# Three-pass scores and a split projection in differential attention, and scores between the two maps' transposes in forgetting attention

## The reference, cut to what matters

```python
def forgetting_attention(q, k, v, fg_logit):        # per head
    s = einsum(q_block, k) * ATT_SCALE + cum[q] - cum[k]
    s = where(ki <= qi, s, NEG)
    out = softmax(s) @ v

def diff_attention(q, k, v, lam):                   # per head: q, k hold two maps of width 64
    sc = einsum(q_block, k) * scale                 # two maps
    p = softmax(where(mask, sc, neg))
    w = p[map 0] - lam * p[map 1]
    out = w @ v
```

## Time and profile before

| what | value |
|---|---|
| median of 3 runs | 2993.35 us (2993.19 to 2996.78) |
| the profiled execution's own time | 2991.64 us |
| its span, first to last instruction | 2990.0 us |
| mean granted TensorE clock | 0.988 |
| PE busy | 2814.2 us, 94% of the span |
| DVE busy | 1602.3 us, 54% |
| ACT busy | 655.7 us, 22% |
| a head of forgetting attention in the loop | 85.66 us |
| a head of differential attention in the loop | 72.96 us |

### The profile page before, as it was taken

How to read it: one execution, slowest core, us unless ns; L and a number is a source line. 1 busy time by engine, 2 the same in 40 slices (tenths; PEclk the granted TensorE clock), 3 DMA queues, 4 the chain that set the end, 5 groups by cost and what they waited for, 6 DMA issues and landing times.

```text
span 2990.0 us, 35245 instructions
## 1 busy us (share of the span) xinstructions
PE 2814.2 (94%) x13336; PEld 2222.8 (74%) x13336; DVE 1602.3 (54%) x2058; ACT 655.7 (22%) x1157; POOL 299.7 (10%) x295
## 2 busy tenths in 40 slices
PE   6889999989999999999999999999998999999996
PEld 4757776868888888877888888888866777777664
DVE  5664446364454555555454554445374666666644
ACT  3133224031111111112110111011032333333321
POOL 0599800000000000001000000000000000000000
PEclk9999999999999999999999999999999999999998
DMA  4211110324343434433222222222242222222131
GB/s 148 85 57 57 42 54 20 138 99 169 112 159 135 154 132 163 154 111 130 83 73 82 83 71 84 84 84 70 85 155 98 72 72 72 70 70 72 52 113 70
DMA packets 48617, 286.59 MB, mean 96 GB/s; under 512 B 6576, under 2 KB 6704, under 8 KB 18608
## 3 DMA queue, kind: packets, MB, share of 16 engines
q1 hardware_dynamic: 22064, 119.01, 11.6%
q0 software_dynamic: 14544, 105.91, 10.2%
q10 hardware_dynamic: 11952, 60.89, 5.3%
HBM read 248.03 MB, written 29.36 MB: 93 GB/s over the span
## 4 chain that ended last, share of the span: by engine, by line
PE 79%; DVE 12%; issue 4%; ACT 2%; DMA 1%; DVEq 0%; SPq 0%; ACTq 0%
PE PB L239 11%; PE PB L241 11%; PE PB L240 11%; PE OBB L239 8%; PE OBB L241 8%; PE OBB L240 8%; PE TBB L754 3%; PE OBB L842 3%; PE PB L800 3%; PE TBB L239 2%; PE TBB L240 2%; PE TBB L241 2%; DVE small L1010 1%; DVE on L1820 1%; DVE cacc L1196 1%
## 5 line engine op out<-in xcount | busy, mean ns | idle before, releaser
L239 PE MATMUL PB<-HH,WH 128*128 128x512 f32 x1520 | 599.9, 395 | 23.9 <-issue 7.7
L241 PE MATMUL PB<-HH,WL 128*128 128x512 f32 x1520 | 595.2, 392 | 0.0
L240 PE MATMUL PB<-HL,WH 128*128 128x512 f32 x1520 | 595.1, 392 | 0.0
L239 PE MATMUL OBB<-HH,WH 128*128 128x512 f32 x992 | 400.0, 403 | 0.9 <-DVE WL L255 0.9
L241 PE MATMUL OBB<-HH,WL 128*128 128x512 f32 x992 | 387.7, 391 | 0.0
L240 PE MATMUL OBB<-HL,WH 128*128 128x512 f32 x992 | 387.0, 390 | 0.0
L239 PEld LDWEIGHTS PB<-HH,WH 128*128 128x128 f32 x1520 | 287.5, 189 | 91.5 <-issue 27.2
L240 PEld LDWEIGHTS PB<-HL,WH 128*128 128x128 f32 x1520 | 287.6, 189 | 61.8 <-issue 2.2
L241 PEld LDWEIGHTS PB<-HH,WL 128*128 128x128 f32 x1520 | 287.1, 189 | 59.7
L255 DVE TENSOR_TENSOR WL<-RAW,WH 128x2048 fp32r<-128x2048 f32 x101 | 234.1, 2318 | 60.8 <-DMA WH<-units 44.1
L2058 POOL DMA_DIRECT2D WH<-units x85 | 45.5, 535 | 2009.6 <-PE PB L239 1320.1
(11 more groups left out here) (314 smaller groups left out, 3743.9 us busy)
## 6 DMA issues: line engine op xcount, KB each, us to landing
WH<-units POOLq DMA_DIRECT2D x85, 1024.0 KB, 5.0
RAW<-units SPq DMA_DIRECT2D x85, 1024.0 KB, 4.7
gs<-units ACTq DMA_DIRECT2D x16, 1024.0 KB, 4.8
gu<-gs ACTq DMA_DIRECT2D x16, 1024.0 KB, 3.9
RAW<-gu SPq DMA_DIRECT2D x16, 1024.0 KB, 4.8
WH<-gu POOLq DMA_DIRECT2D x16, 1024.0 KB, 5.3
tmpd<-xr SPq DMA_DIRECT2D x128, 64.0 KB, 2.0
A<-xT SPq DMA_DIRECT2D x4, 1024.0 KB, 12.5
```

The lines of the kernel that those rows point to most:

```text
L239: first = pe.e.matmul(out, wh, xh, start=start, stop=False)
L240: pe.e.matmul(out, wh, xl, start=False, stop=False)
L241: return pe.e.matmul(out, wl, xh, start=False, stop=stop), first
```

## The change

In differential attention q and k of a head are split into high and low parts (`qh`, `ql`, `kh`, `kl`, float32r), and the scores are three float32r matmuls in place of one float32 matmul, at least 256 columns wide. The copies `qT` and `kT` go; `qh` and `kh` are made by ACT and `ql` and `kl` by DVE (`low_scores`), all in block 7. A part of a projection that ends in a block keeps its last two contraction tiles (6 matmuls, `TAIL`) for a place between `scores(t + 1)` and `values(t)`. ACT copies a projection out of `DB` between the two exponentials; DVE copies a gate after both maxima. The `low_part` at a head's end moves behind `at1`.

In forgetting attention `scores(t + 1)` and the square sums go between the transposes of the first and of the second map; up to block 3 the maps have a bank each. `maximum(t + 1, 0)` goes before the second map's copies, and the norm's Ln and Exp (`root_of`) between the two exponentials.

```diff
@@ scores(t) @@
-                for b in range(0, n, HALF):
+                for b in range(0, n if not forget else 0, HALF):
+                    w = max(256, min(HALF, n - b))
+                    for q_part, k_part in ((qh, kh), (qh, kl), (ql, kh)):
+                        for c in range(2):
+                            rows = slice(64 * c, 64 * c + 64)
+                            pe.e.matmul(PB[c][:, b:b + w], q_part[rows, t * P:(t + 1) * P],
+                                        k_part[rows, b:b + w], start=q_part is qh and k_part is kh,
+                                        stop=False, skip_group_check=True)
+                for b in range(0, n if forget else 0, HALF):
@@ turn(t) becomes turn(t, c) @@
+            def turn_bank(t, c, g):
+                return TB[c if forget and t < 4 else g]
@@ projections @@
+            TAIL = 6
+            def projections(t, tail=False):
                 for part in plan[t]:
                     if not (more or part[0] == "g"):
                         continue
+                    if not forget and t < NB and part[3] == KT:
+                        part = part[:2] + ((TAIL, KT) if tail else (part[2], TAIL))
+                    elif tail:
+                        continue
@@ attend_pe, the block @@
-                turn(t)
-                if forget and more:
-                    for x, h in ended(plan, t, "qk"):
-                        square_sums(pe, x, h, i)
-                        last_evac[0] = f"r{x}{h}"
+                turn(t, 0)
                 if t + 1 < NB:
                     scores(t + 1)
+                projections(t, True)
+                if forget:
+                    if more:
+                        for x, h in ended(plan, t, "qk"):
+                            square_sums(pe, x, h, i)
+                            last_evac[0] = f"r{x}{h}"
+                    turn(t, 1)
                 values(t)
@@ attend_act @@
-                elif block_out:
+                if not forget and more and t == NB - 1:
+                    e.wait_ge(dve_done, at_mark(act, "dve", "q1T", i))
+                    e.activation(qh[:, :], qN[:, :], ACT.Copy, scale=0.125).then_inc(act_done, act.mark("cq"))
+                    e.wait_ge(dve_done, at_mark(act, "dve", "k1T", i))
+                    e.activation(kh[:, :], kN[:, :], ACT.Copy).then_inc(act_done, act.mark("ck"))
+                if t and block_out:
                     block_out(t - 1)
+                if not forget and t + 1 < NB:
+                    exps(t + 1, 0)
                 halves_out(t)
...
                     high_tile(act, early[t])
+                if forget and t + 1 < NB:
+                    exps(t + 1, 0)
+                root_of(t)
                 if t + 1 < NB:
-                    for c in range(2):
-                        exps(t + 1, c)
+                    exps(t + 1, 1)
@@ attend_dve @@
-                out_of_banks(t)
+                out_of_banks(t, 0)
+                if t + 1 < NB:
+                    maximum(t + 1, 0)
+                if forget:
+                    out_of_banks(t, 1)
                 if fill:
                     fill(t)
-                gates(t)
                 if t + 1 < NB:
-                    maximum(t + 1, 0)
                     maximum(t + 1, 1)
+                if not forget:
+                    gates(t)
+                    if more and t == NB - 1:
+                        low_scores(dve, i)
                 outputs(t)
...
+        def low_scores(dve, i):
+            dve.e.wait_ge(act_done, at_mark(dve, "act", "cq", i))
+            dve.e.scalar_tensor_tensor(ql[:, :], qN[:, :], 0.125, qh[:, :].bitcast(F32),
+                                       ALU.mult, ALU.subtract).then_inc(dve_done, dve.mark("ql"))
+            dve.e.wait_ge(act_done, at_mark(dve, "act", "ck", i))
+            dve.e.tensor_tensor(kl[:, :], kN[:, :], kh[:, :].bitcast(F32),
+                                ALU.subtract).then_inc(dve_done, dve.mark("kl"))
@@ diff_dve, behind at1; first_dve makes kh, kl in place of kT @@
-                if not more:
+                if more:
+                    low_part(dve, U_DIFF + 4, i, 2)
+                else:
```

More of the change, by code:

```diff
@@ L723, in build @@
         kN = work("kN", [P, S], F32, 12 * K)
+        qh = work("qh", [P, S], F32R, 0)
+        kh = work("kh", [P, S], F32R, 4 * K)
+        ql = at("ql", [P, S], F32R, 108 * K)
+        kl = at("kl", [P, S], F32R, 28 * K)
         vF = work("vF", [P, S], F32, 16 * K)
@@ L814, in scores, with turn @@
                                     pe_done, pe.mark(f"s{c}_{t}"))
-            def turn(t):
-                if not more and t:
+            def turn_bank(t, c, g):
+                return TB[c if forget and t < 4 else g]
+            def turn(t, c):
+                if not more and t and not c:
                     warm(pe, TB[0], 1 if forget else 2)
[L819 to L832, removed]
+                src = (E0, E1)[c]
+                if forget:
+                    pe.e.wait_ge(act_done, at_mark(pe, "act", f"e{c}_{t}", i))
+                for g in range(1 if t < 4 else 2):
+                    if not forget:
+                        pe.e.wait_ge(dve_done, at_mark(pe, "dve", f"w{t}_{g}", i))
+                        if t:
+                            pe.e.wait_ge(dve_done, at_mark(pe, "dve", f"pt0_{t - 1}_{int(t > 4) * g}", i))
+                    elif t < 4:
+                        if t:
+                            pe.e.wait_ge(dve_done, at_mark(pe, "dve", f"pt{c}_{t - 1}_0", i))
+                    elif c:
+                        pe.e.wait_ge(dve_done, at_mark(pe, "dve", f"pt0_{t}_{g}", i))
+                    else:
+                        pe.e.wait_ge(dve_done, at_mark(pe, "dve", f"pt1_{t - 1}_{g}" if t > 4 else f"pt{g}_3_0", i))
+                    transposes(pe, turn_bank(t, c, g), lambda b: src[:, b * P:(b + 1) * P],
+                               range(4 * g, min(4 * g + 4, t + 1)), f"T{c}_{t}_{g}")
             def values(t):
@@ L952, in exps, with root_of @@
                                  act_done, act.mark(f"e{c}_{t}"))
+            def root_of(t):
+                if forget and more:
+                    for x, h in ended(plan, t, "qk"):
+                        norm_root_act(act, x, h, i)
+                        busy[0] = f"N{x}{h}"
             def halves_out(t):
@@ L996, in attend_act @@
                 e.preload_act_table_set(LN_EXP)
-            if more:
-                e.wait_ge(dve_done, at_mark(act, "dve", "Nq1" if forget else "q1T", i))
+            if more and forget:
+                e.wait_ge(dve_done, at_mark(act, "dve", "Nq1", i))
                 e.activation(qT[:, :], qN[:, :], ACT.Copy, scale=0.125).then_inc(act_done, act.mark("cq"))
@@ L1033, in gates, with out_of_banks @@
                         dve_done, dve.mark(f"rawg{h}"))
[L1035 to L1048, removed]
+            def out_of_banks(t, c):
+                for g in range(1 if t < 4 else 2):
+                    k = min(4, t + 1 - 4 * g)
+                    e.wait_ge(pe_done, at_mark(dve, "pe", f"T{c}_{t}_{g}", i))
+                    if not forget:
+                        e.tensor_tensor(PT0[:, 4 * g:4 * g + k, :],
+                                        TB[g][:, 0:k * P].rearrange("p (b n) -> p b n", n=P),
+                                        rtok[:, 4 * g:4 * g + k].unsqueeze(2).to_broadcast([P, k, P]),
+                                        ALU.mult).then_inc(dve_done, dve.mark(f"pt{c}_{t}_{g}"))
+                        continue
+                    e.tensor_copy((PT0, PT1)[c][:, 4 * g:4 * g + k, :],
+                                  TB[c if t < 4 else g][:, 0:k * P].rearrange("p (b n) -> p b n", n=P)).then_inc(
+                                      dve_done, dve.mark(f"pt{c}_{t}_{g}"))
             def outputs(t):
@@ L1086, in attend_dve @@
             if more:
-                e.wait_ge(dve_done, at_mark(dve, "dve", "Nk1" if forget else "k1T", i))
-                e.tensor_copy(kT[:, :], kN[:, :]).then_inc(dve_done, dve.mark("ck"))
-                low_part(dve, u0 + 4, i, 2)
+                if forget:
+                    e.wait_ge(dve_done, at_mark(dve, "dve", "Nk1", i))
+                    e.tensor_copy(kT[:, :], kN[:, :]).then_inc(dve_done, dve.mark("ck"))
+                    low_part(dve, u0 + 4, i, 2)
+        def low_scores(dve, i):
[5 more added lines that the diff above has]
+                                ALU.subtract).then_inc(dve_done, dve.mark("kl"))
         HEADS = {True: ATT_PAIRS, False: DIFF_HEADS}
@@ L1157, in first_act @@
             act.e.wait_ge(dve_done, at_mark(act, "dve", "Nq1" if forget else "q1T"))
-            act.e.activation(qT[:, :], qN[:, :], ACT.Copy, scale=0.125).then_inc(act_done, act.mark("cq"))
+            act.e.activation((qT if forget else qh)[:, :], qN[:, :], ACT.Copy, scale=0.125).then_inc(
+                act_done, act.mark("cq"))
             if not forget:
+                act.e.wait_ge(dve_done, at_mark(act, "dve", "k1T"))
```

(9 more changed lines are left out.)

10 lines of the change are left out of this document (5 added, 5 removed).

## The result

The changed kernel takes 3040.40 us (median of 4 runs, 3036.62 to 3044.26), the kernel before 2993.61 (4 runs, 2993.19 to 2996.78): ratio 1.0152, 95% interval 1.0139 to 1.0165. It is slower, as forecast, but by 46.8 us and not by 10.5, and outside the range. The profiled execution took 3037.79 us.

A forecast was written before the change was run, and what follows sets the result against it. PE was taken to bound both kinds of loop head, with holes. Terms -12.3 + 0.7 + 1.0 + 17.5 + 3.6 = +10.5 us on the median 2993.35 gave 3003.9 us, range 2984 to 3022.

The forecast's parts named there:

- its four DMAs on SP land 4.45 us after its start: Differential loop head, block 4: after the later copy the DMAs take 4.45 us, so the rotary product holds DVE into block 5.
- 1.75 before block 7's transposes: Differential loop head: block 7's transposes wait 1.75 us for the softmax chain, with 1.36 us less PE work before them.
- 0.6 + 0.9 before the values: Differential loop head: values wait 0.6 us in block 5 and 0.9 in block 6, the rotary product holding DVE.
- 1.25 of the v part: Differential loop head, block 5: the v part waits 1.25 us more, as ACT copies k only after the late exponential.
- 0.7 + 0.5 behind the gates: Differential loop head: stalls of 0.7 us in block 0 and 0.5 in block 1 for DVE's gate copy.
- The 0.2 in each of blocks 2 to 4: Differential loop head: ACT's copy behind the first exponential stalls blocks 2, 3 and 4 by 0.2 us each, 0.6 together.
- the forecast 2.5: Differential loop head: 6.4 us new waits, less 2.5 old gaps and 1.46 of scores, gives +2.5; seven heads +17.5.
- Scores in three passes: Differential heads, blocks 1 to 7: float32r pairs of 0.21 to 0.23 us save 1.46 us a head, bounds 1.1 to 1.6.
- The rival of exposed row halves: Differential scores: exposed weight loads cost 2.3 us a head, 3022; no overlap 3.6 or more, 3035; chance 0.12.
- The price is in `freed()`: Differential heads, kept-back tail: only `values(t)` now covers the copy out of `DB`, 0.3 us in block 0 to 1.8 in block 7.
- Forgetting attention: Forgetting heads: scores hide the first map's copy, 4.1 us gained a head, -12.3 for three; last head +0.7.
- The ends of differential attention: Before the first differential head the split costs +1.0 us; last head +3.6, from `high_tile` in the chain and gate copies.

The follow-up runs named there:

- experiment 1: Changed kernel, with the signal releasing the 1 MB load in the differential loop given by the last product of v0's first part: 3009.61 us, ratio 1.0049.
- 4: Changed kernel without the tail: differential projections run whole ahead of a block's transposes, ScalarE and VectorE orders as changed: 3079.86 us, ratio 1.0284.
- 5: Changed kernel, with ScalarE's copy of the projection ahead of the first map's exponential again in differential heads: 3000.22 us, ratio 1.0018.
- 6: Kernel of experiment 1, with ScalarE's copy ahead of the first exponential in differential heads as well: 2991.84 us, ratio 0.9992.
- 9: Kernel of 7, with one bank for both maps' transposes in blocks 0 to 3: 2983.51 us, ratio 0.9964.
- 12: Kernel of 10, with ScalarE's root of the squares' sums ahead of the first map's exponential: 2978.93 us, ratio 0.9947.
- experiment 3: Kernel before, with only the three-pass differential scores, the split of q and k, and the low part behind the head: 2991.42 us, ratio 0.9991.
- 2: Only the forgetting half of the change; differential heads and VectorE's low part as in the kernel before: 2985.42 us, ratio 0.9964.
- 7: Kernel before, with the forgetting half of the change in its three loop heads alone: 2981.17 us, ratio 0.9949.
- 10: Kernel of 7, with the first map's maximum of the next block behind both maps' copies: 2995.24 us, ratio 1.0000.
- 11: Kernel before, with the 1 MB load in differential loop heads released by block 6's first score product: 2993.67 us, ratio 0.9999.
- 8: Kernel of 7, with three-pass scores in the differential heads, whole projections and old orders there: 2977.78 us, ratio 0.9943.

## Why the prediction missed

**The step that failed** is "its four DMAs on SP land 4.45 us after its start", applied in the walk to k's second half too. The figure came from a place where no large load was near. I had seen that the copy moves later and followed ScalarE, VectorE and SyncE; I didn't follow GpSimd's queue, whose load is released by the v part, and the v part now starts right behind that copy. The missing term is 29.4 us over seven heads (experiment 1), of the 36.3 by which the forecast fell short. The cause is shown from both sides: taken away in the changed kernel it gives the time back; put into the kernel before it delays the same swap by the same amount, and costs nothing, because there the product isn't awaited.

**The rest of the walk held.** With the collision taken away a loop head is 75.7 us (529.78 in seven). The waits of PE in such a head of experiment 1:

```profile
PE TBB L758 <- DVE E L1069: 1.6, 1, 1.6
PE OBB L864 <- DVE PT L1084: 1.1, 2, 0.7
PE OBB L239 <- ACT xr L956: 1.0, 1, 1.0
PE OBB L239 <- DVE sg L1076: 0.9, 2, 0.6
```

These are the forecast's 1.75 before block 7's transposes, 0.6 + 0.9 before the values, 1.25 of the v part and 0.7 + 0.5 behind the gates. The 0.2 in each of blocks 2 to 4 is too short for this view; from the first product of the values to the next projection's first these blocks take 0.85, 0.97 and 1.23 us against 0.64, 0.87 and 1.09 before, 0.45 in all for 0.6.

The total, 2.6 us a head more for the forecast 2.5, is closer than its terms, and that is luck. Counted by starts and gaps, the new waits come to 5.5 us for 6.4, the old ones that went to 1.8 for 2.5, and the scores to 1.3 less for 1.46: the errors cancel. The forecast's own 17.5 for seven heads is a rounded 2.5 taken seven times; unrounded, 2.44, it is 17.1.

**Scores in three passes.** The pairs take 0.23 us, as priced. The rival of exposed row halves is out: loads on the same rows run under the pair before, and the pairs stay 0.22 to 0.24 us apart. With it goes, for these shapes, the Trainium skill's rule ("TensorE: Matmul & The Clock Gate", Part 3, "The mechanism") that weight loads overlap running matmuls only where the row group differs. What I counted too high is what the passes are worth: alone they give 0.5 us a head.

**The tail and the orders.** The price I put on the evacuation was about right, but the text charged it to the tail ("The price is in `freed()`"). Experiments 4 to 6 divide it: the tail softens the order of ScalarE (4: 5.6 us a head worse without it), and the order, copy behind the first exponential, costs 1.5 us a head where nothing collides, and the collision where something can.

**Forgetting attention.** -13.9 for -12.3: right, 4.6 us a head where I had 4.1. The last head's order costs 1.4 us for 0.7; the other 1.6 of its 3.0 goes with the clock. Of the edits in this half only TensorE's order matters (9, 12).

**The ends of differential attention.** In front of the first head the stretch is 1.7 us longer (3.2 in experiment 3) for 1.0. Neither is a clean price: with the old code there it takes 81.5 to 83.0 us over the runs (before, 2, 7, 9 to 12), with the split 83.2 to 84.8 (changed, 1, 3 to 6, 8). The last head +6.3 for +3.6: the right place, since the head is 60.8 us with the copy and `high_tile` ahead of the exponential (5). PE's waits for the weights in the last head, before and after:

```profile
PE TBB L754 <- DVE E L1025: 8.1, 6, 1.6
```

```profile
PE TBB L758 <- DVE E L1067: 11.0, 5, 2.5
```

That is 2.9 us; PE's busy time grows by 3.1 at a granted clock of 0.92 against 1.00, which the sum had no term for. I didn't take the clock apart by an experiment, but the old code of this head takes 60.5 us at 1.00 (before, 2, 9, 12) and 61.9 to 62.1 at 0.97 (7, 10, 11), and the changed code 66.9 at 0.92 and 68.3 at 0.90 (1).

**Everything between the attentions** grew by 1.2 us, which stays open; these stretches differ by up to 5 us over the runs (2016.1 to 2021.4).

## What to carry to other kernels

Before you move the work that frees a bank behind an instruction that waits, ask what that wait is for and who else is released by the bank: here a copy behind an exponential behind a maximum held TensorE's next projection, and in the other half a root did the same. When a transfer's issue or its release moves, list all queues that move with it; a small transfer's landing time holds only for the company in which it was measured. A late transfer costs what its reader waits for, so the same collision may be worth nothing or 4 us.

## What the hardware showed that I had not expected

- A swap of 64 KB issued 0.03 to 0.7 us behind a 1 MB load of another queue lands after 5.5 to 6.3 us in place of 2.0 (changed kernel, 11). Issued 0.2 us ahead of the load it takes 3.8 to 3.9 us, in two heads of seven 5.5 to 5.6 (5); 0.5 us ahead or more, it keeps 1.9 to 2.0. The 1 MB load of `RAW` issued next takes 7.1 us in place of 4.9. In 11 the late swap's packets begin after most of the load's. The Trainium skill ("DMA: Bandwidth & Descriptors", "Queues, rings and completion order") says that an engine serves its queues in turn, a whole packet at a time; that would fit, but the views here don't part the 16 engines.
- Near the end of TensorE's wait of 4.50 us its granted clock fell to 0.50 (1.2 GHz) and stayed there 6.8 us. It fell in all seven heads of the changed kernel (waits of 4.3 to 5.0 us), and in two of them stayed low for 3.4 us only. The waits of 1.6 us at block 7 in experiment 1 didn't bring it down. A head lost 0.4 us on the mean, 0.9 in the head shown, beyond the lateness of its product.
- float32r matmuls of 64 rows pair up over the two row halves as float32 ones do: 0.23 us a pair of 512 columns.
